# Expert layer walked by pairs of units, with a second place for five of the twelve weight panels

## The chip, the cores and the metric

The program runs on one core of one Trainium2 chip. The metric is the time of one execution on the device, in microseconds (us). The number to forecast is the time of the changed kernel beside a median of 2511.3 us for the kernel before.

## The reference, cut to what matters

The program computes three transformer blocks in a row on 256 tokens of width 1024, in float32. The change lies in the second block, in its mixture of experts. Each token picks 4 of 32 experts; an expert is a pair of dense layers with a clipped gate between them:

```
logits = h @ router_w + router_b
top_logit, top_idx = top_k(logits, 4);  gate = softmax(top_logit)
# for each expert e and the tokens that picked it
hid = xb @ w1[e] + b1[e]                  # [tokens, 2048]
glu = minimum(hid[:, :1024], 7.0)
lin = clip(hid[:, 1024:], -7.0, 7.0)
act = glu * sigmoid(1.702 * glu) * (lin + 1.0)
out = (act @ w2[e] + b2[e]) * gate        # summed into each token's row
```

## The kernel before

**Units.** A unit is up to 64 tokens of one expert. Every expert has one unit; an expert with more than 64 tokens gets further units behind the first 32. With these inputs no expert has more, so 32 units run, unit u being expert u. The number of units and their experts are computed on the chip, so each engine first reads a small table, `unit_int`, into a register, and then runs a hardware loop over units (`Fori`).

**Panels.** The weights of an expert are 12 panels of 1 MB each (128 partitions of 8 KB): panels 0 to 7 are `w1`, panels 8 to 11 are `w2`. Each panel has one place: panels 0 to 5 lie in `core.ring`, panels 6 to 11 in `expert_ring`. SyncE (SP) issues all panel transfers, in order, on one queue. For panel j of unit u it waits until TensorE has used panel j of unit u-1 (semaphore `used`), and ahead of each unit it reads the expert's number from the table. TensorE waits for `loaded[j]` ahead of panel j. The twelve panels of expert 0 are fetched earlier, by `load_first`, which SP runs at the end of the block of the output projection (`linear` with `w_out2`); the last four of these wait for that projection's own last panels.

**A unit on TensorE** (line numbers of the profile): the bias (L2599); 32 matmuls with panels 0 to 7 (L2604), 64 tokens as the stationary side, so that two matmuls lie beside each other in the two column halves; `scatter` of the unit before (L2413), which brings the outputs back to their tokens; `gather` of the tokens of the next unit (L2386); turning of the gates (L2613); turning of the hidden values (L2618), which needs a copy by ScalarE to have freed its PSUM bank; bias (L2623), which needs VectorE's first `add`; turning of the gathered tokens (L2392); 16 matmuls with panels 8 to 11 (L2634). After the last unit `scatter` runs once more, and VectorE adds it and updates the residual `x`.

**Scatter before.** `ytok` holds the unit's output with its first 512 columns on partitions 0 to 63 and its last 512 on 64 to 127. `selt` is 128 x 512: the gates stand in the upper left and the lower right block and zeros elsewhere, so four matmuls of 128 rows by 512 columns bring both halves at once, into banks 2 to 5.

**Order.** All order is written by hand. Engines meet at the ends of blocks (`core.block()`), where every engine waits for the others. An fp32 matmul stands in the trace as two records, each with a weight load of its own.

Of the kernel before, what the change touches and what calls it, by code (L numbers as in the profile page):

```python
# [14 lines left out]
P = 128  # L15
TOK = 256
NB = TOK // P
D = 1024
# [2309 lines left out]
def mixture_of_experts(core, h, norm, bias, ring, rw):  # L2328
# [6 lines left out]
    with ExitStack() as s:  # L2335
# [6 lines left out]
        unit_int = sb("unit_int", [1, MAX_UNITS + 1], I32)  # L2342
        selt, ytok = sb("selt", [P, 2 * TOK]), sb("ytok", [P, D // 2])
# [3 lines left out]
        xt, xg, hidt = sb("xt", [P, D // 2]), sb("xg", [P, 4, 2, S]), sb("hidt", [P, D // 2])  # L2347
        glu, lin, sg = sb("glu", [P, D // 2]), sb("lin", [P, D // 2]), sb("sg", [P, D // 2])
        loaded, used = ring.loaded, ring.used
# [6 lines left out]
        scatter_banks = (2, 3, 4, 5)  # L2356

        def unit_count(eng):
            return eng.value_load(unit_int[0:1, MAX_UNITS:MAX_UNITS + 1], min_val=E, max_val=MAX_UNITS)
# [43 lines left out]
        def scatter(pe, u):  # L2403

            pe.wait_ge(copied.sem, copied.at(u))
            pe.wait_ge(gates_copied.sem, gates_copied.at(u))

            pe.wait_ge(added.sem, added.at(u * 4))  # L2410
            for t, bank in enumerate(scatter_banks):

                pe.matmul(ps[:, bank, :], ytok[:, t * P:t * P + P], selt[:, :], start=True, stop=True).then_inc(scattered.sem, 1)  # L2413

        def add(dve, u):
            for t, bank in enumerate(scatter_banks):
                dve.wait_ge(scattered.sem, scattered.at(u * 4 + (t + 1)))
                dve.tensor_tensor(acc[:, t::4, :], acc[:, t::4, :],  # L2418
                                  ps[:, bank, :].rearrange("p (k n) -> p k n", n=TOK), ALU.add).then_inc(added.sem, 1)

        with ExitStack() as s2:
# [9 lines left out]
            row = sb2("row", [1, MAX_UNITS + 1])  # L2431
# [4 lines left out]
            with core.block() as block:  # L2436
# [66 lines left out]
                def _(dve):  # L2503
# [61 lines left out]
                    link(dve.tensor_scalar(row[:, MAX_UNITS:], cum[0:1, E - 1:E], float(E), None, ALU.add))  # L2565
# [10 lines left out]
        with core.block() as block:  # L2576
            @block.sync
            def _(sp):
                n = unit_count(sp)
                with sp.Fori(1, n) as u:  # L2580
                    e = sp.value_load(unit_int[0:1, bass.ds(u, 1)], min_val=0, max_val=E - 1)
                    for j in range(PANELS):

                        sp.wait_ge(used.sem, u * PANELS - (PANELS - 1 - j))
                        sp.dma_start(ring.panel(j), ring.weights(e, j)).then_inc(loaded[j].sem, 16)

            @block.tensor
            def _(pe):
                n = unit_count(pe)
                with pe.Fori(0, n) as u:  # L2590
                    def panel(j):
                        pe.wait_ge(loaded[j].sem, loaded[j].at(u * 16 + 16))
                        return ring.flat(j)
                    pe.wait_ge(expert_picked.sem, expert_picked.at(u + 1))
                    pe.wait_ge(xg_ready.sem, xg_ready.at(u + 1))

                    for bank in range(2):
                        for out, at in halves:
                            pe.matmul(ps[out, bank, :], pick[:, :], bias[:, bank * D + at:bank * D + at + 512], start=True, stop=False)  # L2599
                    for j in range(8):  # L2600
                        w = panel(j)
                        for bank in range(2):
                            for out, at in halves:
                                mm = pe.matmul(ps[out, bank, :], xg[:, j % 4, j // 4, :], w[:, bank * D + at:bank * D + at + 512],  # L2604
                                               start=False, stop=(j == 7))
                        mm.then_inc(used.sem, 1)
                    scatter(pe, u)

                    pe.wait_ge(picked.sem, picked.at(u + 2))
                    gather(pe)  # L2610
                    pe.wait_ge(gates_picked.sem, gates_picked.at(u + 1))
                    for b in range(NB):
                        mm = pe.transpose(ps[:, 7, b * P:b * P + P], selg[:, b, :], ident)  # L2613
                    mm.then_inc(gates_turned.sem, 1)
                    pe.wait_ge(hid_ready.sem, hid_ready.at(u + 1))
                    pe.wait_ge(xt_ready.sem, xt_ready.at(u + 2))
                    for c in range(4):
                        mm = pe.transpose(ps[:, 6, c * P:c * P + P], lin[:, c * P:c * P + P], ident)  # L2618
                    mm.then_inc(hid_turned.sem, 1)

                    pe.wait_ge(added.sem, added.at(u * 4 + 1))
                    for out, at in halves:
                        mm = pe.matmul(ps[out, 2, :], pick[:, :], bias[:, 2 * D + at:2 * D + at + 512], start=True, stop=False)  # L2623
                    mm.then_inc(bias_used.sem, 1)
                    pe.wait_ge(gates_copied.sem, gates_copied.at(u + 1))
                    turn_gathered(pe, u + 2)
                    pe.wait_ge(hid_copied.sem, hid_copied.at(u + 1))
                    for q in range(4):
                        w = panel(8 + q)
                        for i in range(2):  # L2630
                            k = 2 * q + i
                            at_k = k % 4 * P + k // 4 * S
                            for out, at in halves:
                                mm = pe.matmul(ps[out, 2, :], hidt[:, at_k:at_k + S], w[:, i * D + at:i * D + at + 512],  # L2634
                                               start=False, stop=(k == DT - 1))
                        mm.then_inc(used.sem, 1)
                scatter(pe, n)

            @block.scalar
            def _(act):  # L2640
                n = unit_count(act)
                with act.Fori(0, n) as u:
                    act.wait_ge(glu_ready.sem, glu_ready.at(u + 1))
                    act.activation(sg[:, :], glu[:, :], ACT.Sigmoid, scale=SWIGLU_ALPHA).then_inc(sig_ready.sem, 1)  # L2644
                    copy_gathered(act, u + 2)
                    act.wait_ge(hid_turned.sem, hid_turned.at(u + 1))
                    act.activation(hidt[:, :], ps[:, 6, :], ACT.Copy).then_inc(hid_copied.sem, 1)
                    copy_turned(act, u + 2)

            @block.vector  # L2650
            def _(dve):
                n = unit_count(dve)
                with dve.Fori(0, n) as u:
                    link = LoopChain(turn, dve, u, 5)

                    dve.wait_ge(gathered.sem, gathered.at(u + 1))
                    pick_tokens(dve, link, u + 1)
                    dve.wait_ge(used.sem, used.at(u * PANELS + 8))
                    dve.tensor_scalar(glu[:, :], ps[:, 0, :], SWIGLU_LIMIT, None, ALU.min).then_inc(glu_ready.sem, 1)  # L2659
                    link(dve.tensor_scalar(lin[:, :], ps[:, 1, :], SWIGLU_LIMIT, -SWIGLU_LIMIT, ALU.min, ALU.max))  # L2660
                    dve.wait_ge(glu_ready.sem, glu_ready.at(u + 1))
                    link(dve.scalar_tensor_tensor(out=lin[:, :], in0=lin[:, :], scalar=1.0, in1=glu[:, :], op0=ALU.add,
                                                  op1=ALU.mult))
                    dve.wait_ge(sig_ready.sem, sig_ready.at(u + 1))
                    link(dve.tensor_tensor(lin[:, :], lin[:, :], sg[:, :], ALU.mult))
                    dve.sem_inc(hid_ready.sem, 1)
                    dve.wait_ge(gates_turned.sem, gates_turned.at(u + 1))
                    dve.tensor_copy(selt[0:S, 0:TOK], ps[0:S, 7, 0:TOK])
                    dve.tensor_copy(selt[S:P, TOK:], ps[S:P, 7, 0:TOK]).then_inc(gates_copied.sem, 1)
                    add(dve, u)  # L2670
                    pick_gates(dve, link, u + 1)
                    dve.wait_ge(bias_used.sem, bias_used.at(u + 1))
                    pick_expert(dve, u + 1)
                    dve.wait_ge(used.sem, used.at(u * PANELS + 12))
                    dve.tensor_copy(ytok[:, :], ps[:, 2, :]).then_inc(copied.sem, 1)  # L2675
                    link.done()
# [653 lines left out]
```

## Time and profile before

| what | value |
|---|---|
| median of three runs | 2511.3 us (2507.07 to 2517.31) |
| the profiled execution's own time | 2518.12 us |
| its span, first to last instruction | 2515.1 us |
| TensorE busy | 2374.4 us, 94% of the span |
| VectorE, ScalarE, GpSimd busy | 680.9, 411.7, 66.0 us |
| mean granted TensorE clock | 0.975 of full speed |
| moved from HBM | 616.63 MB, 246 GB/s over the span |

The time is that of an execution, the span lies within it, 3 us shorter. Busy shares are means over stages of quite different kinds: three blocks of dense layers, and between about 1275 and 2234 us the expert loop, some 38% of the whole. A share of the whole span says nothing of what limits the loop; that is read from windows within it.

### The profile page before, as it was taken

How to read it: one execution, taken by the hardware profiler on the slowest of the kernel's cores; microseconds unless marked ns; L12 is line 12 of the kernel's file. 1: busy time of each engine (PE TensorE's matmuls, PEld its weight loads, DVE VectorE, ACT ScalarE, POOL GpSimd, SP SyncE). 2: the span in 40 equal slices, each digit the busy share in tenths (PEclk: the TensorE clock that was granted, in tenths of full speed). 3: DMA queues.
4: the chain of work that ended last, by engine and by line, in shares of the span. 5: the costliest groups of instructions: out<-in, count | busy, mean ns of one | idle time of the engine just before them, and what ended most of it. 6: DMA issues, size and time to landing. Idle time of an engine off the chain costs nothing. (4 is left out here: it accounts for less than half of the span.)

```text
span 2515.1 us, 31570 instructions
## 1 busy us (share of the span) xinstructions
PE 2374.4 (94%) x12727; PEld 1548.0 (62%) x12727; DVE 680.9 (27%) x1486; ACT 411.7 (16%) x837; POOL 66.0 (3%) x72
## 2 busy tenths in 40 slices
PE   8999999999999998997789999999999999989998
PEld 7778788886788877875633333333333333348787
DVE  3142100025200024525222232222222222242322
ACT  2210100014100013223311111111111111112331
POOL 0110000000000000011200000000000000000000
PEclk9999999999999999998789999999999999989999
DMA  6333544455744444300569999999999999952422
GB/s 258 117 117 134 201 151 142 159 201 218 284 167 147 146 159 159 118 19 1 222 242 417 418 418 418 418 417 417 417 417 418 418 418 417 418 224 92 152 76 91
DMA packets 105015, 619.00 MB, mean 246 GB/s; under 512 B 9856, under 2 KB 11136, under 8 KB 48128
## 3 DMA queue, kind: packets, MB, share of 16 engines
q1 hardware_dynamic: 103216, 611.10, 62.1%
q10 hardware_dynamic: 1712, 6.63, 0.7%
q8 instruction: 69, 1.13, 0.2%
q14 instruction: 18, 0.15, 0.0%
HBM read 616.63 MB, written 1.05 MB: 246 GB/s over the span
## 5 line engine op out<-in xcount | busy, mean ns | idle before, releaser
L391 PE MATMUL ps<-x_res,ring 128*128 128x256 f32 x2560 | 568.2, 383 | 21.6 <-ACT x_res L953 12.9
L391 PEld LDWEIGHTS ps<-x_res,ring 128*128 128x128 f32 x2560 | 488.2, 192 | 97.7 <-issue 22.4
L2604 PE MATMUL ps<-ring,moe_xg 128*64 128x512 f32 x1536 | 336.9, 595 | 0.0
L391 PE MATMUL ps<-first_arena,ring 128*128 128x256 f32 x1088 | 239.4, 379 | 0.5 <-DMA ring<-w_o_dram 0.5
L2604 PEld LDWEIGHTS ps<-ring,moe_xg 128*64 128x64 f32 x1536 | 110.7, 137 | 208.4 <-issue 202.9
L2634 PE MATMUL ps<-expert_ring,moe_hidt 128*64 128x512 f32 x1024 | 226.8, 595 | 0.0
L391 PEld LDWEIGHTS ps<-first_arena,ring 128*128 128x128 f32 x1088 | 206.6, 190 | 29.0 <-DMA ring<-w_o_dram 1.0
L391 PE MATMUL ps<-third_h,ring 128*128 128x256 f32 x768 | 176.6, 387 | 5.2 <-ACT third_h L274 3.9
L391 PEld LDWEIGHTS ps<-third_h,ring 128*128 128x128 f32 x768 | 147.7, 194 | 28.2 <-issue 6.5
L2634 PEld LDWEIGHTS ps<-expert_ring,moe_hidt 128*64 128x64 f32 x1024 | 70.5, 137 | 133.5 <-issue 133.5
L2659 DVE TENSOR_SCALAR moe_glu<-ps 128x512 f32<-128x512 f32 x32 | 22.2, 692 | 417.4 <-PE ps L2604 417.4
L2644 ACT ACTIVATE moe_sg<-moe_glu 128x512 f32<-128x512 f32 x32 | 20.1, 629 | 637.2 <-DVE moe_glu L2659 637.2
L2413 PE MATMUL ps<-moe_selt,moe_ytok 128*128 128x512 f32 x264 | 122.1, 605 | 0.9 <-DVE moe_ytok L2675 0.9
L2604 PE MATMUL ps<-expert_ring,moe_xg 128*64 128x512 f32 x512 | 115.3, 592 | 0.0
L391 PE MATMUL ps<-mix_arena,ring 128*128 128x256 f32 x416 | 96.5, 390 | 3.9 <-ACT mix_arena L274 3.9
L1330 DVE TENSOR_TENSOR first_arena<-first_arena,ps 128x256 f32<-128x256 f32 x44 | 18.5, 421 | 286.7 <-PE ps L391 286.7
L2413 PEld LDWEIGHTS ps<-moe_selt,moe_ytok 128*128 128x128 f32 x264 | 47.4, 189 | 75.1 <-issue 75.1
L391 PEld LDWEIGHTS ps<-mix_arena,ring 128*128 128x128 f32 x416 | 79.9, 195 | 17.2 <-issue 5.7
L2418 DVE TENSOR_TENSOR moe_acc<-moe_acc,ps 128x512 f32<-128x512 f32 x132 | 82.1, 683 | 2.8 <-PE ps L2413 1.8
L2604 PEld LDWEIGHTS ps<-expert_ring,moe_xg 128*64 128x64 f32 x512 | 36.8, 137 | 73.1 <-issue 73.1
L2675 DVE COPY moe_ytok<-ps 128x512 f32<-128x512 f32 x32 | 22.1, 692 | 176.1 <-PE ps L2634 176.1
L2386 PE MATMUL ps<-moe_ht,moe_sel 128*64 128x512 f32 x264 | 65.7, 619 | 1.6 <-DVE moe_sel L2365 1.6
(522 smaller groups left out, 1985.5 us busy)
## 6 DMA issues: line engine op xcount, KB each, us to landing
expert_ring<-w_dram SPq DMA_DIRECT2D x192, 1024.0 KB, 15.1
ring<-w_dram SPq DMA_DIRECT2D x192, 1024.0 KB, 15.9
ring<-w_in_dram SPq DMA_DIRECT2D x55, 1024.0 KB, 4.9
ring<-ffn_up_dram SPq DMA_DIRECT2D x44, 1024.0 KB, 4.9
ring<-ada_dram SPq DMA_DIRECT2D x36, 1024.0 KB, 4.9
ring<-w_out_dram SPq DMA_DIRECT2D x16, 1024.0 KB, 4.9
ring<-ffn_dn_dram SPq DMA_DIRECT2D x16, 1024.0 KB, 4.9
ring<-ple_g_dram SPq DMA_DIRECT2D x8, 1024.0 KB, 7.0
```

Source lines behind the costliest of these rows:

```text
L391: mm = pe.matmul(core.ps[:, t % BANKS, 0:TOK], w[:, k * PANEL + c * P:k * PANEL + c * P + P], sources[panel](k0 + k), start=(k0 + k == 0), ...
L1330: return e.tensor_tensor(h[:, j, :], h[:, j, :], ps, ALU.mult)
L2386: mm = pe.matmul(ps[out, 6, :], sel[:, b, :], ht[:, b, at:at + 512], start=(b == 0), stop=(b == NB - 1))
L2413: pe.matmul(ps[:, bank, :], ytok[:, t * P:t * P + P], selt[:, :], start=True, stop=True).then_inc(scattered.sem, 1)
L2418: dve.tensor_tensor(acc[:, t::4, :], acc[:, t::4, :], ps[:, bank, :].rearrange("p (k n) -> p k n", n=TOK), ALU.add).then_inc(added.sem, 1)
L2604: mm = pe.matmul(ps[out, bank, :], xg[:, j % 4, j // 4, :], w[:, bank * D + at:bank * D + at + 512], start=False, stop=(j == 7))
L2634: mm = pe.matmul(ps[out, 2, :], hidt[:, at_k:at_k + S], w[:, i * D + at:i * D + at + 512], start=False, stop=(k == DT - 1))
L2644: act.activation(sg[:, :], glu[:, :], ACT.Sigmoid, scale=SWIGLU_ALPHA).then_inc(sig_ready.sem, 1)
L2659: dve.tensor_scalar(glu[:, :], ps[:, 0, :], SWIGLU_LIMIT, None, ALU.min).then_inc(glu_ready.sem, 1)
L2675: dve.tensor_copy(ytok[:, :], ps[:, 2, :]).then_inc(copied.sem, 1)
```

## The change

- A loop turn now handles two units, an even and an odd one. The number of turns is the number of units halved and rounded up (three more small operations on VectorE while routing); an odd count would be filled up with an empty unit.
- Panels 0 to 4 have two places, one for even and one for odd units (`expert_ring` grows by five panels). The other seven keep one place.
- `load_first` also fetches panels 0 to 4 of expert 1, as its last five transfers.
- SP's order of transfers: for the units up to 17, panels 0 to 4 of unit u+1 go ahead of panels 5 to 11 of unit u; from there on in the order in which they are used. For the first 32 units SP takes the expert from its loop counter and reads no table.
- `scatter` is eight matmuls of 64 rows by 256 columns without the zeros, four for each row half, each half into banks of its own. `selt` is half as wide and is copied by one VectorE operation instead of two. `add` is four operations as before, on other slices.
- `hidt`, `glu`, `lin` and `sg` now lie in the memory of `h` (`mix2_y`), which is no longer needed there.

```diff
 def add(dve, u):
-    for t, bank in enumerate(scatter_banks):
-        dve.wait_ge(scattered.sem, scattered.at(u * 4 + (t + 1)))
+    for n, (q, i) in enumerate(((0, 0), (0, 1), (1, 0), (1, 1))):
+        part = acc[:, 4 * i + 2 * q:4 * i + 2 * q + 2, :]
...
 # scatter
-            for t, bank in enumerate(scatter_banks):
-                pe.matmul(ps[:, bank, :], ytok[:, t * P:t * P + P], selt[:, :], start=True, stop=True).then_inc(scattered.sem, 1)
+            for t in range(4):
+                for i, (rows, _) in enumerate(halves):
+                    mm = pe.matmul(ps[:, 2 + 2 * i + t // 2, t % 2 * TOK:t % 2 * TOK + TOK], ytok[rows, t * P:t * P + P],
+                                   selt[rows, :], start=True, stop=True)
+                    if t % 2 == 1:
+                        mm.then_inc(scattered.sem, 1)
...
 # routing
-                    link(dve.tensor_scalar(row[:, MAX_UNITS:], cum[0:1, E - 1:E], float(E), None, ALU.add))
+                    link(dve.tensor_scalar(pairs, cum[0:1, E - 1:E], float(E), 0.5, ALU.add, ALU.mult))
+                    link(dve.tensor_scalar(pairs, pairs, 0.25, ROUND, ALU.add, ALU.add))
+                    link(dve.tensor_scalar(pairs, pairs, ROUND, None, ALU.subtract))
+                    link(dve.tensor_scalar(row[:, MAX_UNITS + 1:], pairs, -1.0, None, ALU.add))
...
 # SP
-                with sp.Fori(1, n) as u:
-                    e = sp.value_load(unit_int[0:1, bass.ds(u, 1)], min_val=0, max_val=E - 1)
-                    for j in range(PANELS):
-                        sp.wait_ge(used.sem, u * PANELS - (PANELS - 1 - j))
-                        sp.dma_start(ring.panel(j), ring.weights(e, j)).then_inc(loaded[j].sem, 16)
+                def load(u, turn, panels, odd, e):
+                    for j in panels:
+                        sp.wait_ge(used.sem, turn * PANELS + (j + 1))
+                        sp.dma_start(ring.panel(j, odd), ring.weights(e, j)).then_inc(ring.loaded_at(j, odd).sem, 16)
+                twice, once = range(TWICE), range(TWICE, PANELS)
+                with sp.Fori(1, AHEAD) as v:
+                    load(v * 2, v * 2 - 2, twice, 0, v * 2)
+                    load(v * 2 - 1, v * 2 - 2, once, 1, v * 2 - 1)
+                    load(v * 2 + 1, v * 2 - 1, twice, 1, v * 2 + 1)
+                    load(v * 2, v * 2 - 1, once, 0, v * 2)
+                def in_turn(v, before, even, odd):
+                    load(v * 2 - 1, v * 2 - 2, once, 1, before)
+                    load(v * 2, v * 2 - 2, twice, 0, even)
+                    load(v * 2, v * 2 - 1, once, 0, even)
+                    load(v * 2 + 1, v * 2 - 1, twice, 1, odd)
+                with sp.Fori(AHEAD, E // 2 - 1) as v:
+                    in_turn(v, v * 2 - 1, v * 2, v * 2 + 1)
...
-PANELS = 12
+PANELS, TWICE, AHEAD = 12, 5, 9
...
 # load_first
+        for j in range(TWICE):
+            sp.dma_start(self.panel(j, 1), self.weights(1, j)).then_inc(self.loaded_at(j, 1).sem, 16)
```

On SP, in the block ahead of the routing, stand the transfers of `load_first` (its first two lines are panels 6 and 7, then 8 to 11, then 0 to 5). Before:

```order
L2717 DMA expert_ring<-w_dram 128x2048 x2
L2717 DMA expert_ring<-w_dram 128x2x1024 x4
L2717 DMA ring<-w_dram 128x2048 x6
L364 UNCONDITIONAL_BRANCH
L2577 UNCONDITIONAL_BRANCH
```

And now:

```order
L2762 DMA expert_ring<-w_dram 128x2048 x2
L2762 DMA expert_ring<-w_dram 128x2x1024 x4
L2762 DMA ring<-w_dram 128x2048 x6
L2764 DMA expert_ring<-w_dram 128x2048 x5
L364 UNCONDITIONAL_BRANCH
L2587 UNCONDITIONAL_BRANCH
```

Five transfers stand between the last one that waits for the projection and the end of the block (L364).

On TensorE, the first half of a unit in the loop: bias, panels 0 to 7, `scatter` (L2413), `gather` (L2386). Before:

```order
L2599 MATMUL ps<-bias_parts,moe_pick 64x512 x4
L2592 ISA
L2604 MATMUL ps<-ring,moe_xg 64x512 x24
L2604 MATMUL ps<-expert_ring,moe_xg 64x512 x8
L2410 ISA
L2413 MATMUL ps<-moe_selt,moe_ytok 128x512 x4
```

And now, the odd unit of a turn (bias L2633, panels L2638, `scatter` L2414):

```order
L2633 MATMUL ps<-bias_parts,moe_pick 64x512 x4
L2638 MATMUL ps<-expert_ring,moe_xg 64x512 x20
L2626 ISA
L2638 MATMUL ps<-ring,moe_xg 64x512 x4
L2638 MATMUL ps<-expert_ring,moe_xg 64x512 x8
L2410 ISA
L2414 MATMUL ps<-moe_selt,moe_ytok 128x256 x8
```

The odd unit reads its first five panels (20 matmuls) from `expert_ring`; in the scatter, eight matmuls of 256 columns stand where four of 512 stood.

## Rows read from the trace of the kernel before

**Rows 1.** Timeline of TensorE, one unit: start us, us, engine line op.
```profile
1336.98 10.47 PE L2604 MATMUL ps<-ring,moe_xg 128*64 128x512 f32 x48
...
1350.82 3.70 PE L2413 MATMUL ps<-moe_selt,moe_ytok 128*128 128x512 f32 x8
1354.45 1.94 PE L2386 MATMUL ps<-moe_ht,moe_sel 128*64 128x512 f32 x8
1356.31 0.44 PE L2613 MATMUL ps<-mat,moe_selg 128*128 128x128 f32 x2
1357.17 0.63 PE L2618 MATMUL ps<-mat,moe_lin 128*128 128x128 f32 x4 [0.42 <-ACT moe_xt L2397]
1358.42 0.41 PE L2623 MATMUL ps<-bias_parts,moe_pick 96*64 96x512 bf16 x2 [0.62 <-DVE moe_acc L2418]
...
1359.35 7.09 PE L2634 MATMUL ps<-expert_ring,moe_hidt 128*64 128x512 f32 x32
...
1366.70 10.47 PE L2604 MATMUL ps<-ring,moe_xg 128*64 128x512 f32 x48
```

**Rows 2.** Windows: stretch, us, busy of PE, PEld, DVE, ACT, POOL; PEclk; DMA share; GB/s.
```profile
1280.00:1290.00 10.00, 10.00 (x49) 3.55 (x47) 0.00 (x0) 0.00 (x0) 0.00 (x0) 1.00 0.93 359
...
1300.00:1330.00 30.00, 28.96 (x130) 10.19 (x132) 8.25 (x20) 3.97 (x6) 0.00 (x0) 1.00 0.95 379
...
1400.00:1500.00 100.00, 96.88 (x436) 33.78 (x431) 24.39 (x55) 11.11 (x15) 0.00 (x0) 1.00 1.02 417
...
2210.00:2220.00 10.00, 9.17 (x36) 3.18 (x32) 4.06 (x7) 1.61 (x3) 0.00 (x0) 1.00 0.88 351
```

**Rows 3.** DMA view of 1320 to 1360 us: KB each, median us to landing.
```profile
ring<-w_dram SPq DMA_DIRECT2D x6, 1024.0 KB, 10.6
```

**Rows 4.** DMA view of 2150 to 2198 us, the same columns.
```profile
ring<-w_dram SPq DMA_DIRECT2D x8, 1024.0 KB, 21.2
```

**Rows 5.** Timeline of TensorE, a pair of 64-row matmuls of 256 columns in the first block.
```profile
572.82 0.60 PE L1085 MATMUL ps<-first_arena 64*128 64x256 f32 x4
573.35 2.86 PE L391 MATMUL ps<-x_res,ring 128*128 128x256 f32 x12
```

**Rows 6.** Timeline of the last unit and of what follows it.
```profile
2219.46 2.48 DVE L2418 TENSOR_TENSOR moe_acc<-moe_acc,ps 128x512 f32<-128x512 f32 x4
...
2221.13 7.09 PE L2634 MATMUL ps<-expert_ring,moe_hidt 128*64 128x512 f32 x32
...
2229.09 3.69 PE L2413 MATMUL ps<-moe_selt,moe_ytok 128*128 128x512 f32 x8 [0.87 <-DVE moe_ytok L2675]
2230.24 0.69 DVE L2418 TENSOR_TENSOR moe_acc<-moe_acc,ps 128x512 f32<-128x512 f32 x1 [1.29 <-PE ps L2413]
...
2232.82 0.69 DVE L2418 TENSOR_TENSOR moe_acc<-moe_acc,ps 128x512 f32<-128x512 f32 x1 [0.17 <-PE ps L2413]
```

**Rows 7.** Timeline around the end of the block ahead of the routing.
```profile
1232.70 2.06 SPq L2717 DMA_DIRECT2D ring<-w_dram  x4
1232.71 0.48 DVE L2250 SCALAR_TENSOR_TENSOR x_res<-ps,modulations,x_res 128x256 f32<-128x256 f32 x1 [2.97 <-PE ps L391]
...
1235.60 0.17 DVE L530 SCALAR_TENSOR_TENSOR norm_gain<-modulations,vec 128x8 f32<-128x8 f32 x1 [2.40 <-PEq L364]
```

**Rows 8.** Timeline at the end of the routing and at the loop's entry.
```profile
1271.82 0.14 DVE L2565 TENSOR_SCALAR route_row<-route_cum 1x1 f32<-1x1 f32 x1
1271.99 0.18 DVE L2566 CAST moe_unit_int<-route_row 1x49 int32<-1x49 f32 x1
...
1274.87 1.06 PE L2599 MATMUL ps<-bias_parts,moe_pick 96*64 96x512 bf16 x4 [3.35 <-issue]
```

**Rows 9.** Window of the first block in which TensorE waited and the transfers were saturated, columns as in rows 2.
```profile
620.00:640.00 20.00, 17.70 (x194) 12.29 (x187) 5.36 (x18) 5.34 (x14) 0.00 (x0) 1.00 1.00 397
```

**Rows 10.** The page's DMA queues: packets, MB, share of 16 engines.
```profile
q8 instruction: 69, 1.13, 0.2%
```

**Rows 11.** DMA queues of 1400 to 1600 us; this one alone moves anything there.
```profile
q1 hardware_dynamic: 14771, 83.53, 101.7%
```

More of the change, by code:

```diff
@@ L2587, in _ @@
+                last = sp.value_load(unit_int[0:1, MAX_UNITS + 1:MAX_UNITS + 2], min_val=E // 2 - 1, max_val=MAX_UNITS // 2 - 1)
+                load(last * 2 + 1, last * 2, once, 1, expert(last * 2 + 1))
             @block.tensor
             def _(pe):
[L2589 to L2601, printed above, removed]
+                n = pair_count(pe)
@@ new lines, in _, with panel @@
+                with pe.Fori(0, n) as v:
+                    for odd in range(2):
+                        u = v * 2 + odd
+                        def panel(j):
+                            sig = ring.loaded_at(j, odd)
+                            pe.wait_ge(sig.sem, sig.at((v if j < TWICE else u) * 16 + 16))
+                            return ring.flat(j, odd)
+                        pe.wait_ge(expert_picked.sem, expert_picked.at(u + 1))
+                        pe.wait_ge(xg_ready.sem, xg_ready.at(u + 1))
@@ L2621, in _ @@
[L2621 to L2636, printed above, removed]
@@ L2637, in _ @@
-                scatter(pe, n)
+                                pe.matmul(ps[out, bank, :], pick[:, :], bias[:, bank * D + at:bank * D + at + 512], start=True, stop=False)
+                        for j in range(8):
+                            w = panel(j)
+                            for bank in range(2):
+                                for out, at in halves:
+                                    mm = pe.matmul(ps[out, bank, :], xg[:, j % 4, j // 4, :], w[:, bank * D + at:bank * D + at + 512],
+                                                   start=False, stop=(j == 7))
+                            mm.then_inc(used.sem, 1)
@@ new lines, in _ @@
+                        for c in range(4):
+                            mm = pe.transpose(ps[:, 6, c * P:c * P + P], lin[:, c * P:c * P + P], ident)
+                        mm.then_inc(hid_turned.sem, 1)
+                        pe.wait_ge(added.sem, added.at(u * 4 + 1))
+                        for out, at in halves:
+                            mm = pe.matmul(ps[out, 2, :], pick[:, :], bias[:, 2 * D + at:2 * D + at + 512], start=True, stop=False)
+                        mm.then_inc(bias_used.sem, 1)
@@ L2639, in _ @@
+                scatter(pe, n * 2)
             @block.scalar
             def _(act):
[L2641 to L2648, printed above, removed]
+                n = pair_count(act)
@@ L2650, in _ @@
             @block.vector
             def _(dve):
[L2652 to L2675, printed above, removed]
```

120 lines of the change are left out of this document (85 added, 35 removed).

## The prediction

> **What bounds the kernel now.** I read the page first. Its busy shares say 94% for TensorE, but over the whole span that is a mean of unlike stages, so I went to the expert loop alone, where the diff works: first its windows, then the timeline of one unit, then the DMA view at an early and at a late stretch.
>
> The windows show both sides of the loop full: TensorE busy 96.88 of 100 us at the full clock, DMA share 1.02 at 417 GB/s [rows 2]. Only one of them can set the pace, and the timeline says which. A unit takes 1366.70 - 1336.98 = 29.72 us, and in it TensorE waits for ScalarE (0.42) and VectorE (0.62), never for a panel [rows 1]. So the loop runs at TensorE's pace. The transfers are slower than that: 83.53 MB in 200 us is 417.65 GB/s [rows 11], so a panel of 1.0486 MB takes 2.511 us and twelve take 30.13 us, 0.41 us more than a unit. The DMA view confirms it: a panel lands 10.6 us after its issue early on and 21.2 us after it at the end [rows 3, 4], and 28 units (from the middle of the one stretch to that of the other) by 0.41 make 11.5. A panel's place comes free a whole unit before the panel is needed again, so this growing delay never reached TensorE in 32 units. DMA is the second limit, 1.4% behind the first: whatever TensorE gains is worth only what DMA lets through. That sets the method: find when the last panel would land, and what TensorE must do after it.
>
> **The transfers.** Before: the windows give a start of transfers at 1290 - 3.59 MB/417.65 GB/s = 1281.4 and an end at 2210 + 8.4 = 2218.4, with 30 - 27.2 = 2.8 us empty between 1300 and 1330 [rows 2]. From the count, 1281.4 + 2.8 + 372 x 2.511 = 2218.2, so the price of a panel holds over the loop. After the change 367 panels are left, five having been fetched in a stretch that has no transfers. The first new transfer still waits for TensorE's first use of panel 0, so the start stays. The 2.8 us hole came from panels 8 to 11, whose places come free late in unit 0; now five panels for unit 2, which have a place at once, stand ahead of them in the queue, so I take the hole as filled. Afterwards SP's next panel always has a free place: with DMA setting the pace, a single place is free when its unit ends, some 15 us after the landing of panel 7, and its next transfer begins 20 us or more after that landing. The loop's 921.4 us of transfers run through.
>
> **Scatter.** It takes 1354.45 - 1350.82 = 3.63 us now [rows 1]. The new form, 64 rows by 256 columns in fp32, one matmul per row half, does occur in this trace: four records, a pair of matmuls, take 573.35 - 572.82 = 0.53 us with the switch to the next form [rows 5]. A 512-column matmul of the old kind takes 3.63/4 = 0.91, so 256 columns one after the other would be 0.45 each and 0.91 a pair; 0.53 shows the halves running beside each other. Four pairs cost between 4 x 0.43 (half of the old work, 0.85 us being the 512-column step without its share of the switch) and 4 x 0.53, so 1.7 to 2.1; I take 1.85, nearer the lower end, because the switch is paid once. Gain 1.78. VectorE then needs one copy instead of two ahead of the first add, and the 0.62 us wait at L2623 shrinks by 0.43. From the start of scatter to L2634 the time goes from 1359.35 - 1350.82 = 8.53 to 6.32 us, the unit from 29.72 to 27.5. That is below the 30.13 of DMA. TensorE starts with a lead of about 17 us at panel 5 (unit 1's panel 5 is the sixth in the new order and lands at 1281.4 + 6 x 2.511 = 1296.5; TensorE, 2.2 us earlier than before, wants it at 1336.98 - 29.72 - 2.2 + 5 x 1.73 = 1313.7), loses 2.6 us of it in each unit, and waits for panels from about unit 8 on. Of the 2.2 x 32 = 71 us that scatter takes off TensorE, most turn into such waits.
>
> **The end of the loop.** The last panel lands at 1281.4 + shift + 921.4. Panel 7 lands four panels earlier (10.04); after it TensorE needs 1.73 for the panel (13.84 us for eight, by the starts at 1336.98 and 1350.82 [rows 1]), 6.32 to L2634 and 7.09 for L2634. Panels 8 to 11 land meanwhile and hold nothing up. So L2634 ends 5.1 us after the last landing. It now ends at 2221.13 + 7.09 = 2228.2 [rows 6]. Behind it, last scatter and adds take 2232.82 + 0.69 - 2229.09 = 4.42; now the first add can again begin after 1.15 (two pairs instead of one matmul of twice the width), and four adds take 2.48 [rows 6]: 3.6, a gain of 0.8.
>
> **What the change costs ahead of the loop.** SP's last four transfers of `load_first` are released by the projection's last panel and take until 1232.70 + 2.06 = 1234.76. VectorE is done at 1233.19, yet the next block starts at 1235.60 [rows 7]: the block's end waits for SP. Five more issues stand there, at (2.06 - 0.35)/3 = 0.57 us each (0.35 for the last one's own length, my estimate), so 2.9 us on the path. If the meeting of the engines hid them it would be 0; at 2.06/3 each it would be 3.4. I take 2.9, since the three moments fit nothing else. Three more linked operations on one element at 1271.99 - 1271.82 = 0.17 [rows 8] add 0.5. Together a shift of 3.4 us for all that follows. The five panels land while nothing else is fetched, 25 us before unit 1.
>
> **Parts at nothing.** SP's table reads: each panel lands 10 to 21 us after issue [rows 3, 4], so SP is that far ahead; without that cover a read would stand between two panels. The half as wide clearing of `selt` on GpSimd ends long before the loop. New memory for `hidt`, `glu`, `lin`, `sg`: same operations. The order for units up to 17 changes which panel is waited for, not how many come: a gap saved there is spent before the end.
>
> **The sum.** Last landing 1281.4 + 3.4 + 921.4 = 2206.2; end of L2634 2211.3 against 2228.2, -16.9; tail -0.8; together -17.7 us. The profiled execution took 2518.1, so 2500.4 for it; it was 6.8 us above the median of the runs shown, so I put the same difference to the median: 2511.3 - 17.7 = **2493.6 us**.
>
> **The rivals.**
> *Transfers get slower* (the other side). All now hangs on the price of a panel, which was covered before. With deeper queues and no slack, every 1% costs 9.2 us. At 2.559 us a panel (410 GB/s) the gain is gone; at the 397 GB/s of a saturated stretch of the first block [rows 9] a panel takes 2.641, and 367 x 0.130 = 48 us more give 2541. Against it: rate and share stayed the same in this loop while the landing time doubled.
> *The doubled loop body no longer stays in instruction memory.* TensorE's turn holds 256 records before and 544 after (two units, eight more each), and a fetch of instructions is 1.13 MB/69 = 16 KB [rows 10]. Before, none is fetched in the loop [rows 11]. A stall of s at each of 16 turns is hidden up to 60.3 - 55 = 5 us once DMA sets the pace, but TensorE alone would end at 2228.2 + 3.4 - 71 + 16 s: from s = 3.2 on it costs, 4.2 takes the whole gain, and 6 gives 2511.3 + 28.4 - 0.8 = 2539. The whole entry to the loop, table read included, shows 3.35 us [rows 8], so even that bound costs little: 2497.
> The Trainium skill's page Runtime: NRT & Kernel Launch, section Instruction fetch mechanics, speaks against the change here: a taken branch to code outside a window of two pages must fetch its page before going on. It also gives TensorE room for 2048 instructions, by which 544 would fit and s would be 0; no row here shows either.
> *The clock falls in the waits.* TensorE will wait 2.6 us in each 30. At half clock a unit would take 55 us, 25 over DMA's time, so two such units would make the kernel slower, ten would give about 2740. In a stretch with the same kind of waits, TensorE busy 17.70 of 20 us, the granted clock was 1.00 [rows 9].
> The page TensorE: Matmul & The Clock Gate, section Loop structure matters more than you think, warns that waits for DMA between bursts send the clock to half; the row above speaks against it for waits this short.
> *The row halves don't overlap.* Then the unit falls by 0.43 only, to 29.3, TensorE stays the bound, and the end is 2228.2 + 3.4 - 14 = 2217.6: -10.6, 2500.7, no measurable change.
> *More gain.* The issues of SP off the path give 2490.7; a panel 1% cheaper, which a queue that is never short could bring, 2484.4.
>
> **How the numbers follow.** Chances: forecast 0.66; slower transfers 0.10; refetching 0.05; clock 0.03; no overlap 0.05; more gain 0.11. A measurement of this kernel tells 0.5%, 12.6 us, from no change, and -17.7 is only 5 us beyond that, half a percent of the panel's price, so a fifth of the likeliest case may fall short: same 0.20. Faster 0.69, slower 0.11. The range 2479 to 2509 holds the forecast with a panel's price 1% off either way, the case without overlap and most of the gain cases, and leaves out the slow ones.
>
> **What would show it.** In the changed profile: DMA share 1.02 at about 418 GB/s from 1285 to 2206 without the dip near 1300; units of 27.5 us at first and of 30.1 from about the eighth on, with waits for panels under 1 us each and the clock at 1.00; scatter at 1.85 us; the last landing near 2206 and L2634's end 5 us later; the block after `load_first` starting near 1238.5. I am wrong if the rate in the loop is under 414 GB/s, if TensorE never waits for panels, or if a gap of several us opens once per turn.

## The result and the profile after

The changed kernel took a median of 2500.65 us (11 runs, 2496.9 to 2504.47) beside 2516.35 us for the kernel before (11 runs, 2507.07 to 2521.91). The ratio is 0.9934, with a 95% interval from 0.9923 to 0.9944: 14 to 19 us less, 16.6 by the ratio and 15.7 by the medians. It is faster by 0.56 to 0.77%. The forecast was 17.7 us less. Its 2493.6 us lies 7 us under the measured time: 5 of these come from the kernel before, which had a median of 2511.3 us in the three runs shown and 2516.35 in eleven, and 2 from a gain that is 2 us smaller by the medians.

The page of the changed kernel, span and costliest groups of the loop (line, engine, names, count, busy time and mean, idle time before them and what ended it):

```profile
span 2501.1 us, 31823 instructions
...
q8 instruction: 71, 1.16, 0.2%
...
L2638 PE MATMUL ps<-expert_ring,moe_xg 128*64 128x512 f32 x1152 | 262.4, 596 | 24.6 <-DMA expert_ring<-w_dram 24.4
...
L2638 PE MATMUL ps<-ring,moe_xg 128*64 128x512 f32 x896 | 202.9, 598 | 15.5 <-DMA ring<-w_dram 14.9
```

The first of the two groups on the page of the kernel before (the second has 0.0 idle time there too):

```profile
L2604 PE MATMUL ps<-ring,moe_xg 128*64 128x512 f32 x1536 | 336.9, 595 | 0.0
```

TensorE is now idle for 40.1 us ahead of its panels, and 39.3 of these are waits that the landing of a panel ends. Before there was none. The windows, with the columns of [rows 2]:

```profile
1280.00:1290.00 10.00, 10.00 (x42) 3.40 (x40) 0.00 (x0) 0.00 (x0) 0.00 (x0) 0.88 0.58 211
...
1300.00:1330.00 30.00, 29.46 (x152) 11.19 (x152) 9.96 (x24) 4.33 (x7) 0.00 (x0) 1.00 0.99 393
1400.00:1500.00 100.00, 95.42 (x481) 35.30 (x478) 28.63 (x64) 12.26 (x18) 0.00 (x0) 1.00 1.02 417
2200.00:2210.00 10.00, 9.14 (x52) 4.21 (x54) 6.12 (x13) 2.42 (x4) 0.00 (x0) 1.00 0.95 381
```

The rate of the transfers in the middle of the loop is what it was. The timeline of TensorE, first an early unit, then a late one (in brackets the idle time before a row and what ended it):

```profile
1322.30 2.00 PE L2414 MATMUL ps<-moe_selt,moe_ytok 64*128 64x256 f32 x16
1324.22 1.94 PE L2386 MATMUL ps<-moe_ht,moe_sel 128*64 128x512 f32 x8
...
1327.64 0.41 PE L2657 MATMUL ps<-bias_parts,moe_pick 96*64 96x512 bf16 x2
...
1328.56 7.09 PE L2668 MATMUL ps<-expert_ring,mix_y 128*64 128x512 f32 x32
...
1574.42 1.94 PE L2638 MATMUL ps<-ring,moe_xg 128*64 128x512 f32 x8 [0.94 <-DMA ring<-w_dram]
1576.90 1.94 PE L2638 MATMUL ps<-expert_ring,moe_xg 128*64 128x512 f32 x8 [0.55 <-DMA expert_ring<-w_dram]
1579.42 1.94 PE L2638 MATMUL ps<-expert_ring,moe_xg 128*64 128x512 f32 x8 [0.58 <-DMA expert_ring<-w_dram]
...
1604.57 1.94 PE L2638 MATMUL ps<-ring,moe_xg 128*64 128x512 f32 x8 [0.91 <-DMA ring<-w_dram]
```

Scatter lasts 1.92 us by its starts (3.63 in [rows 1]), VectorE's wait at L2657 is gone, and from scatter to L2668 it is 6.26 us. Late, a unit takes 1604.57 - 1574.42 = 30.15 us, with three waits for panels in it, at the last three of the eight; an early one takes 27.45 us. The first wait for a panel comes at 1458.78, in unit 6 counted from 0. The last unit and what follows, the counterpart of [rows 6]:

```profile
2200.38 1.94 PE L2638 MATMUL ps<-expert_ring,moe_xg 128*64 128x512 f32 x8 [0.56 <-DMA expert_ring<-w_dram]
...
2208.52 7.09 PE L2668 MATMUL ps<-expert_ring,mix_y 128*64 128x512 f32 x32
2216.47 2.00 PE L2414 MATMUL ps<-moe_selt,moe_ytok 64*128 64x256 f32 x16 [0.87 <-DVE moe_ytok L2712]
```

And the end of the block ahead of the routing with the loop's entry, the counterpart of [rows 7, 8]:

```profile
1235.72 0.48 DVE L2250 SCALAR_TENSOR_TENSOR x_res<-ps,modulations,x_res 128x256 f32<-128x256 f32 x1 [2.97 <-PE ps L391]
1237.71 2.63 SPq L2764 DMA_DIRECT2D expert_ring<-w_dram  x5
1240.87 0.17 DVE L530 SCALAR_TENSOR_TENSOR norm_gain<-modulations,vec 128x8 f32<-128x8 f32 x1 [4.66 <-PEq L364]
...
1278.80 1.06 PE L2633 MATMUL ps<-bias_parts,moe_pick 96*64 96x512 bf16 x4 [3.93 <-issue]
```

Ahead of all that the diff touches, this execution is already 3.0 us behind the one of before (the last L2250 at 1235.72 against 1232.71). The code there is the same, and in the profiles of the experiments this point moves between 1225.7 and 1237.3, so all comparisons of traces start from it. From it to L2668's end the changed kernel takes 979.89 us, the one before 995.51: -15.6. The tail adds -0.8 (the four adds now end 3.65 us after the last scatter begins, 4.42 before). With -0.6 us behind these adds and the +3.0 ahead, that is the -14.0 between the spans.

### The profile page after: what moved, and what is told of

Its sections match the earlier page's. It is cut to its first block and busy times, and to the rows that moved or that the text cites. A ratio compares the mean times of both kernels' runs of the same rounds, so it can differ in the third digit from the quotient of the medians.

```text
span 2501.1 us, 31823 instructions
## 1 busy us (share of the span) xinstructions
PE 2333.7 (93%) x12991; PEld 1541.4 (62%) x12991; DVE 664.8 (27%) x1457; ACT 391.4 (16%) x821; POOL 65.9 (3%) x72
## 5 line engine op out<-in xcount | busy, mean ns | idle before, releaser
L2638 PE MATMUL ps<-expert_ring,moe_xg 128*64 128x512 f32 x1152 | 262.4, 596 | 24.6 <-DMA expert_ring<-w_dram 24.4
L2668 PE MATMUL ps<-expert_ring,mix_y 128*64 128x512 f32 x1024 | 226.8, 595 | 0.0
L2638 PE MATMUL ps<-ring,moe_xg 128*64 128x512 f32 x896 | 202.9, 598 | 15.5 <-DMA ring<-w_dram 14.9
L2638 PEld LDWEIGHTS ps<-expert_ring,moe_xg 128*64 128x64 f32 x1152 | 77.9, 136 | 198.3 <-issue 126.3
L2668 PEld LDWEIGHTS ps<-expert_ring,mix_y 128*64 128x64 f32 x1024 | 70.6, 137 | 133.4 <-issue 133.4
L2638 PEld LDWEIGHTS ps<-ring,moe_xg 128*64 128x64 f32 x896 | 62.6, 137 | 146.0 <-issue 103.9
L2697 DVE TENSOR_SCALAR mix_y<-ps 128x512 f32<-128x512 f32 x32 | 22.1, 692 | 473.1 <-PE ps L2638 473.1
L2680 ACT ACTIVATE mix_y<-mix_y 128x512 f32<-128x512 f32 x32 | 20.2, 630 | 713.9 <-DVE mix_y L2697 713.9
L2414 PEld LDWEIGHTS ps<-moe_selt,moe_ytok 64*128 64x128 f32 x528 | 48.3, 186 | 32.1 <-issue 27.7
L2386 PE MATMUL ps<-moe_ht,moe_sel 128*64 128x512 f32 x264 | 65.7, 619 | 1.6 <-DVE moe_sel L2365 1.6
L2414 PE MATMUL ps<-moe_selt,moe_ytok 64*128 64x256 f32 x528 | 65.9, 389 | 0.9 <-DVE moe_ytok L2712 0.9
```

The source lines that it names most:

```text
L2386: mm = pe.matmul(ps[out, 6, :], sel[:, b, :], ht[:, b, at:at + 512], start=(b == 0), stop=(b == NB - 1))
L2414: mm = pe.matmul(ps[:, 2 + 2 * i + t // 2, t % 2 * TOK:t % 2 * TOK + TOK], ytok[rows, t * P:t * P + P], selt[rows, :], start=True, stop=True)
```

## The experiments

**The scatter alone, and the places and order alone.** The first kernel is the kernel before with nothing but the new scatter (its matmuls, its copy of `selt` and its `add`):

```diff
-        selt, ytok = sb("selt", [P, 2 * TOK]), sb("ytok", [P, D // 2])
+        selt, ytok = sb("selt", [P, TOK]), sb("ytok", [P, D // 2])
...
-                pe.matmul(ps[:, bank, :], ytok[:, t * P:t * P + P], selt[:, :], start=True, stop=True).then_inc(scattered.sem, 1)
+                for i, (rows, _) in enumerate(halves):
+                    mm = pe.matmul(ps[:, 2 + 2 * i + t // 2, t % 2 * TOK:t % 2 * TOK + TOK], ytok[rows, t * P:t * P + P],
+                                   selt[rows, :], start=True, stop=True)
...
```

> The kernel before with the new scatter, selt copy and add only: one place for each panel, no extra panels fetched early, single units. If the loop is now set by transfers (my theory), 372 panels still have to land by about 2218 us, so the gain is only what lies behind the last landing: 2218.4 + 6.5 against 2228.2, and 0.8 in the tail, about -4 us against the kernel before (ratio 0.998), with TensorE waiting for panels in late units. Rival 1: scatter is the whole gain and the second places are idle: -16 us. Rival 2: with one place for each panel the waits of TensorE hold places back and the transfers tear: no gain or slower.

Measured 2510.44 us, ratio 0.9971 (0.9961 to 0.9981): -7.3 us, 3 us more than I had put down. Its trace shows 1.4 of these: between 1290 and 1330 us 1.2 us of transfers are missing, in the kernel before 2.6. The rest is within the interval. The lines of TensorE in its loop:

```profile
L2609 PE MATMUL ps<-ring,moe_xg 128*64 128x512 f32 x1532 | 346.2, 597 | 17.0 <-DMA ring<-w_dram 13.8
...
L2609 PE MATMUL ps<-expert_ring,moe_xg 128*64 128x512 f32 x504 | 120.4, 602 | 27.8 <-DMA expert_ring<-w_dram 27.8
```

So it waits for panels like the changed kernel, with single places. The second kernel is the changed one with the old scatter (the same edit the other way round).

> The changed kernel with the old scatter (four matmuls of 128 rows by 512 columns, two selt copies). My theory: TensorE sets the pace again at 29.7 us a unit, panels fetched early buy nothing, and what remains is the price ahead of the loop, some 2.3 us for five issues and 1 us in routing and loop entry: +3 us against the kernel before (ratio 1.001). Rival: the second places and the new order shorten the loop by themselves: -12 us.

Measured 2518.51 us, ratio 1.0002 (0.9993 to 1.0011), with no wait for a panel in the loop. The +3 us that I had expected is not there: the loop's entry lies 43.09 us behind the last L2250, 42.16 in the kernel before, because the block behind the longer gap is shorter (see the last section). Alone the places and the order bring nothing; alone the scatter brings 7.3 us; together they bring 16.6. With the old scatter TensorE sets the pace, and five panels fewer in the loop are worth nothing. With the new one the transfers set it, and those five (5 x 2.51 = 12.6 us) lie on the path. The step from the scatter alone to both is 9.3 us by the ratios and 10.8 by the traces to the end of L2668, less than 12.6: the transfers start 0.6 us later, 0.5 us more are missing near 1300, and what is left would be a slightly higher price of a panel.

**Where the five extra transfers are issued.** The third kernel issues them ahead of the six that wait for the projection:

```diff
-        for j in [*range(RING, PANELS), *range(RING)]:
...
+        for j in range(RING, PANELS):
             sp.dma_start(self.panel(j), self.weights(0, j)).then_inc(self.loaded[j].sem, 16)
         for j in range(TWICE):
             sp.dma_start(self.panel(j, 1), self.weights(1, j)).then_inc(self.loaded_at(j, 1).sem, 16)
+        for j in range(RING):
+            sp.wait_ge(core.panel_used.sem, core.panel_used.at(range(j, total, RING)[-1] + 1))
+            sp.dma_start(self.panel(j), self.weights(0, j)).then_inc(self.loaded[j].sem, 16)
```

> The changed kernel, but load_first issues the five panels of expert 1 ahead of the six that wait for the projection instead of behind them. My theory: the block's end waited for those five issues, and the whole rest of the program moves up by their 2.3 us: -18 us against the kernel before, 2.3 us less than the changed kernel. Rival: the block's end waits for something else, or the early transfers hold back the bias and router loads: same as the changed kernel, about -15.7.

Measured 2498.33 us, ratio 0.9927 (0.9913 to 0.994). By the time alone, 1.8 us less by the ratios, it can't be told from the changed kernel (0.9923 to 0.9944). The trace does tell: from the last L2250 to the next block 1236.33 - 1234.05 = 2.28 us, against 5.15 after and 2.89 before. The entry comes 3.0 us earlier (40.05 us behind the last L2250, 43.08 after) and the end of L2668 3.6 us earlier. The fourth kernel goes further: the six panels of the ring are issued in the routing's block, where nothing has to be waited for; `load_first` issues only the other eleven.

```diff
+    def load_more(self, sp):
+        for j in range(RING):
+            sp.dma_start(self.panel(j), self.weights(0, j)).then_inc(self.loaded[j].sem, 16)
...
+                @block.sync
+                def _(sp):
+                    ring.load_more(sp)
```

> As the run before, and in addition the six panels of expert 0 that go into ring are issued without a wait in the routing block, so that SP is done early in the projection's block. My theory: the block's end then waits for VectorE alone (1233.2 + 0.35 in the trace of before, where it was 1235.6): 2 us more, -20 us against the kernel before. The six panels need 15 us and have 40. Rival: the issues in the routing block or their transfers delay the loop's entry: no better than -16.

Measured 2493.4 us, ratio 0.9909 (0.9894 to 0.9925), the fastest version: 6.3 us less than the changed kernel by the ratios, whose intervals just touch. Its timeline:

```profile
1232.96 0.48 DVE L2250 SCALAR_TENSOR_TENSOR x_res<-ps,modulations,x_res 128x256 f32<-128x256 f32 x1 [2.97 <-PE ps L391]
1233.80 2.98 SPq L2767 DMA_DIRECT2D ring<-w_dram  x6
1233.84 0.17 DVE L530 SCALAR_TENSOR_TENSOR norm_gain<-modulations,vec 128x8 f32<-128x8 f32 x1 [0.40 <-PEq L364]
...
1234.38 3.72 PE L517 MATMUL ps<-mix_y,mat 128*128 128x256 f32 x16 [1.46 <-ACT mix_y L524]
```

The gap is 0.88 us, and L517's 16 records take 3.72 us instead of 5.40. From the last L2250 to the loop's entry (1270.30) it is 37.34 us, against 43.08 after: 4.3 from the gap, 1.5 from the block behind it, where TensorE's clock stood higher in L517 (see the last section). Inside the loop 0.9 us is lost again (937.75 us from the entry to the end of L2668, 936.81 after).

**The order of the transfers.** The fifth kernel fetches in order of use from the start, the sixth keeps the order by free places up to unit 3 instead of up to unit 17 (AHEAD = 2 instead of 9). The edit of the fifth:

```diff
-                with sp.Fori(1, AHEAD) as v:
-                    load(v * 2, v * 2 - 2, twice, 0, v * 2)
-                    load(v * 2 - 1, v * 2 - 2, once, 1, v * 2 - 1)
-                    load(v * 2 + 1, v * 2 - 1, twice, 1, v * 2 + 1)
-                    load(v * 2, v * 2 - 1, once, 0, v * 2)
...
-                with sp.Fori(AHEAD, E // 2 - 1) as v:
+                with sp.Fori(1, E // 2 - 1) as v:
```

> The changed kernel with SP's loads in order of use from unit 1 on; two places and the five panels fetched early stay. My theory: the order is worth what it does at the start. The first load is now panel 5 of unit 1, whose place comes free five panels (8.7 us) later than that of panel 0, and panels 8 to 11 are again waited for late in unit 0 (2 to 3 us empty): about +11 us against the changed kernel, -5 against the kernel before. Rival: transfers catch up, because only their total counts and the order costs nothing: -16.

Measured 2509.85 us, ratio 0.9967 (0.9956 to 0.9979): +8.3 us beside the changed kernel. Entry and SP's first rows:

```profile
1275.05 1.07 PE L2627 MATMUL ps<-bias_parts,moe_pick 96*64 96x512 bf16 x4 [3.89 <-issue]
...
1288.00 0.35 SPq L2593 DMA_DIRECT2D ring<-w_dram  x1
```

Panel 5 of unit 1 stands first now, and its place comes free only after TensorE's panel 5: SP starts 12.95 us after the entry instead of 1283.09 - 1278.80 = 4.29. That is 8.7 us. The second part of the expectation is there too: from 1290 to 1330 us 4.4 us of transfers are missing, 1.7 after. By the traces, from the last L2250 to the last L2668's end, the loss is 11.5 us (991.41 against 979.89), the sum of the two. The 8.3 us of the ratios is lower, but their intervals leave about 4 us either way.

> The changed kernel with the order by free places for units up to 3 only (AHEAD 2), in order of use from there. My theory: the order counts only at the start, so this is the changed kernel, -16 us against the kernel before. Rival: the order keeps the transfers full through the first 17 units: several us slower.

Measured 2506.06 us, ratio 0.9956 (0.9942 to 0.997). I had expected no loss; the rival of my expectation came true. A window and SP's row show it:

```profile
1340.00:1360.00 20.00, 19.52 (x104) 7.70 (x102) 6.66 (x14) 2.42 (x4) 0.00 (x0) 1.00 0.76 294
...
1343.07 0.37 SPq L2593 DMA_DIRECT2D ring<-w_dram  x1
```

At the switch SP stood at panel 5 of unit 3, which has one place, until 1343.07, when TensorE had used it. At 294 GB/s the window is 20 x (1 - 294/417) = 5.9 us short of full, and the loss is 5.9 by the traces to L2668's end and 5.5 by the ratios. The changed kernel issues past the same switch at 1757.5 us, when TensorE already waits for panels and the transfers lie some 20 us behind their issue, and no window of 20 us between 1760 and 1820 falls below 415 GB/s.

**How many panels have two places.** Two instead of five (TWICE = 2), so 370 panels in the loop instead of 367, and three issues fewer ahead of it.

> The changed kernel with two places for panels 0 and 1 only, and two panels fetched early. My theory: each panel fetched early is worth its 2.51 us and costs one issue of 0.46 us ahead of the routing, so three fewer give +7.5 - 1.4 = +6.1 us against the changed kernel, -10 against the kernel before; with two panels ahead the hole near 1300 us may be deeper, 1 to 2 us more. Rival: it is the second place that keeps the transfers running, and fewer of them cost much more than their own transfers: +15 or more.

Measured 2508.46 us, ratio 0.9964 (0.9954 to 0.9974): +7.6 beside the changed kernel, and 3 x 2.51 = 7.5. The gap at the block's end fell to 3.68 us, but the entry stayed where it was (43.11 us behind the last L2250, 43.08 after), so the 1.4 us that I had set against the 7.5 did not come, and neither did a deeper hole near 1300.

**The table reads.** SP reads the expert of each unit from the table again, as before.

```diff
+                    before, even, odd = expert(v * 2 - 1), expert(v * 2), expert(v * 2 + 1)
...
```

> The changed kernel, but SP reads the experts' numbers from the table in every loop turn. My theory: SP runs 10 to 20 us ahead of the landings, so nothing changes: -16 us against the kernel before. Only the reads ahead of the first load could show, and they lie within the wait for TensorE's first panel. Rival: reads leave holes between transfers: some 1 us for each of 15 turns, +15.

Measured 2502.25 us, ratio 0.9938 (0.9919 to 0.9956). No difference to the changed kernel that can be measured, and SP's first issue follows the entry by 4.30 us, 4.29 after.

**Which of the two sets the pace.** The last two kernels take work off one side each. The first leaves out half of the scatter's matmuls:

```diff
-            for t in range(4):
+            for t in (1, 3):
```

> The changed kernel with the odd two of the four pairs of scatter's matmuls alone (each about 0.48 us in a unit of TensorE): half of the outputs are left out. Theory, the transfers set the pace after about the seventh unit: TensorE's work in the middle of the loop is covered, and only what it leaves out behind the last landing counts, 1 us in the last unit and 1 us in the last scatter; the waits for panels grow by 1 us a unit. About -2 us beside the changed kernel, 2498, -18 beside the kernel before. Rival, TensorE's work still counts in each unit: 32 x 1 us, 2469.

Measured 2498.48 us, ratio 0.9921 (0.9895 to 0.9947). The interval holds the changed kernel's ratio and is far from the 0.98 of the rival. Entry to L2668's end takes 934.43 us, against 936.81 after, although each unit has 0.9 us less to do. Of these 2.4 us about 1 is the last unit's own, as expected, and 1.4 are the smaller hole near 1300 (0.3 us of transfers missing, 1.7 after). Its late units show where the rest of the saving went:

```profile
2157.46 1.94 PE L2638 MATMUL ps<-ring,moe_xg 128*64 128x512 f32 x8 [0.23 <-DMA ring<-w_dram]
...
2187.62 1.94 PE L2638 MATMUL ps<-expert_ring,moe_xg 128*64 128x512 f32 x8 [0.25 <-DMA expert_ring<-w_dram]
```

These are two units, 30.16 us apart as before, each now with five waits instead of four in the same late units (panel 3's, shown, is the new one). In all, TensorE waits 61.0 us for panels, 39.3 after.

The second fetches only half of each panel in the loop, the other half stays that of an earlier expert:

```diff
+                        place, source = ring.panel(j, odd), ring.weights(e, j)
+                        if j < 8:
+                            place, source = place[:, 0:1024], source[:, 0:1024]
+                        else:
+                            place, source = place[:, 0:1, :], source[:, 0:1, :]
...
```

> The changed kernel with only half of each panel fetched in the loop (half of the weights are those of an earlier expert), so the same number of transfers, waits and issues with half the bytes. Theory, the price of a panel is the bytes and it alone sets the pace: TensorE never waits for a panel, its units stay at 27.45 us to the end, and the loop ends at 1279 + 32 x 27.45 = 2157 us in place of 2215: about -57 us beside the changed kernel, 2444, ratio to the kernel before 0.971. Rival, the waits come from something else in the transfers (their issue by SP, the hand-over of places): units stay near 30.1 us and the time near 2500. Rival, TensorE's own pace is slower than the early units show when all their panels lie there: anything between.

Measured 2438.6 us, ratio 0.9697 (0.9656 to 0.9737). The last unit, a window, and the lines of the loop:

```profile
2141.86 7.09 PE L2673 MATMUL ps<-expert_ring,mix_y 128*64 128x512 f32 x32
...
1400.00:1500.00 100.00, 98.56 (x496) 36.66 (x496) 25.75 (x62) 10.69 (x16) 0.00 (x0) 1.00 0.67 225
...
L2643 PE MATMUL ps<-expert_ring,moe_xg 128*64 128x512 f32 x1152 | 255.3, 592 | 0.0
```

No wait for a panel is left, with the same number of transfers, issues and hand-overs. Entry (1268.59) to L2673's end (2148.95) takes 880.4 us, 27.5 for each of 32 units; the 56.4 us to the changed kernel's 936.8 are what its waits for bytes cost. That is more than the 40.1 of idle time on the page, because a wait costs more than its idle time: with a wait ahead of each panel, TensorE takes a panel every 1.94 + 0.55 = 2.49 us instead of 1.73, which is 0.76 for a wait of 0.55.

## Why the prediction was right, and where it was not

**Right.** Halving the bytes removed all waits; halving the scatter moved L2668's end by 2.4 us and otherwise only lengthened the waits. Scatter cost 1.92 us (1.85). Table reads cost nothing that can be measured. The moved buffers were not tested alone, but the units took what was forecast with them. The three more operations on one element cost 0.5. The waits began in unit 6, where the forecast had about unit 8.

**The terms, from the last L2250 on.** They are worked out from the bytes of windows of one trace of each kernel. The last landing is at 2209.1 (if the window 2200 to 2210 is full up to there), the first transfer starts at 1290 - 2.11 MB/417 GB/s = 1284.95. The last landing came 12.3 us earlier than before, against 12.2 in the forecast, but by other numbers:

| term, us against before | forecast | measured |
|---|---|---|
| start of the transfers | +3.4 | +0.5 |
| five panels fewer | -12.6 | -12.6 |
| hole near 1300 | -2.8 | -1.1 |
| price of a panel (2.514 for 2.511) | 0 | +1.0 |
| L2668's end behind the last landing | -4.7 | -3.3 |
| tail | -0.8 | -0.8 |
| sum | -17.7 | -16.4 |

(The terms are rounded, and the forecast's own count of the transfers before ended 0.2 us under the end that it read, so the columns add up to -17.5 and -16.3.) The sum is close partly by luck: the start came out 2.9 us cheaper than forecast, and hole, price and end together 4.1 us dearer.

*Start, mis-sized.* The five issues of SP lengthened the gap at the block's end by 2.26 us (2.9 forecast): each took 0.57, but SP was done only 2.57 us later than before, and the hand-over behind it was 0.31 us shorter. Then TensorE ran through L517 and the router's matmuls 1.9 us faster than before, at a higher clock, and gave most of it back. The 0.5 us of the three operations came as forecast, and SP's first issue followed the loop's entry 0.4 us sooner (4.29 us for 4.66). The forecast had neither the 1.9 nor the 0.4.

*Hole, partly wrong.* "I take the hole as filled" failed: 1.7 us are missing, most of them here:

```profile
1305.00:1310.00 5.00, 5.00 (x28) 1.80 (x26) 1.19 (x4) 0.00 (x0) 0.00 (x0) 1.00 0.89 273
```

The five panels for unit 2 fill 12.6 us, and the ninth transfer would start at 1284.95 + 8 x 2.51 = 1305.0. It is panel 8 of unit 1, whose place TensorE frees at about 1301.1 + 1.7 = 1302.8. SP issues it at 1303.23, and the first transfer started 1.86 us after its issue (1283.09 to 1284.95), which gives 1305.1 here: the margin is gone. With half a scatter, when TensorE reaches L2668 0.8 us earlier behind the entry, the window 1300 to 1330 has 413 GB/s and 0.3 us are missing. That fits a hole, not its size, and no run was made for this alone.

*End, mis-sized.* The 5.1 us of the forecast left no time between the last byte of panel 7 and its first use. That landing is at 2209.1 - 10.05 = 2199.05 and TensorE begins at 2200.38: 1.33 us.

**Wrong in its reason.** "The order for units up to 17 changes which panel is waited for, not how many come: a gap saved there is spent before the end" was put at nothing. A gap in the transfers is not got back, even when it falls into the early units in which TensorE still sets the pace, because the transfers set the end; and the order decides whether there is one: 11.5 us by the trace (8.3 by the ratios) in order of use from the start, 5.9 (5.5) with the switch at unit 3. The number came out right only because the forecast had SP never waiting for a place, which is what this order achieves.

**The rivals.** *Slower transfers*: the panel's price rose by 0.003 us, a tenth of a percent. *Refetching of the doubled body*: no gap per turn; the page has 71 packets of instructions against 69 in [rows 10], one of the two comes between 1295 and 1325 us, in the first turn, and from 1400 to 2200 us queue q8 moves nothing. The rule of the Trainium skill that spoke against the change (page Runtime: NRT & Kernel Launch, section Instruction fetch mechanics) has no effect visible here at 544 records a turn. *Clock in the waits*: 1.00 with 2.1 us of waits for panels in 30. The warning in the Trainium skill about long waits for DMA between matmuls (page TensorE: Matmul & The Clock Gate, section Loop structure matters more than you think) did not come true for waits of at most 0.94 us. *No overlap of row halves*: 0.48 us a pair, so they overlap. *More gain*: its first half, SP's issues off the path, is real, and the fourth kernel has it. Its second half, a cheaper panel, did not come.

## What to carry to other kernels

When two limits lie 1.4% apart, a large saving on the first is soon cut off by the second: the scatter's 2.2 us in each of 32 units, 71 us of TensorE, gave 7.3 alone. Work out both ends, the last landing and what must follow it, and the gain is their sum. Then every byte and every gap in the second limit is on the path: prefetch during stretches that fetch nothing, and order transfers by free places until the queue leads. From there the order of use did no harm; whether going back to it is needed, no run tests. Transfers issued by an engine at the end of a block hold up all engines: put them into the next block if nothing there needs them at once.

## What the runs showed of the hardware

The block between L530 and the loop's entry does the same work in all kernels, but for 0.5 us of operations, and its length goes with the length of the stop ahead of it. Gap from the last L2250 to L530, TensorE's idle time before L517, time of L517, and L530 to the entry:

| kernel | gap | idle | L517 | block |
|---|---|---|---|---|
| before | 2.89 | 3.46 | 6.53 | 39.27 |
| ring issued in routing | 0.88 | 1.46 | 3.72 | 36.46 |
| extra issued early | 2.28 | 2.85 | 5.14 | 37.77 |
| two panels twice | 3.68 | 4.26 | 6.12 | 39.43 |
| after | 5.15 | 5.72 | 5.40 | 37.93 |

The six other kernels with a gap of 5.1 to 5.3 have blocks of 37.9 (37.85 to 37.90), and the scatter alone, with before's gap, has 39.3. The windows over L517 alone, first of the version with the ring issued in routing, then of before and of after, give the granted clock (third figure from the right, in parts of 2.4 GHz):

```profile
1234.38:1238.10 3.72, 3.72 (x16) 2.95 (x16) 0.00 (x0) 2.09 (x7) 1.94 (x3) 1.00 1.04 390
```

```profile
1236.10:1242.60 6.50, 6.47 (x16) 4.95 (x16) 0.00 (x0) 2.13 (x7) 2.18 (x3) 0.56 1.02 425
```

```profile
1241.40:1246.80 5.40, 5.40 (x16) 4.19 (x16) 0.00 (x0) 2.10 (x7) 1.94 (x3) 0.68 1.03 428
```

After 1.46 us idle TensorE kept its full 2.4 GHz through L517; in the others it stood at 1.2 for most of it. The router's matmuls behind it took 8.70 us at 0.50 before (from 1246.57) and 7.90 us at 0.56 after (from 1250.71). Up to 3.5 us of idle time L517 got slower with the length of the stop, at 4.3 and 5.7 quicker again. Why is open; no run tests it. It moves the block by up to 3 us here, as much as the term that it followed.

Row halves of 64 rows by 256 columns in fp32 cost 1.92/4 = 0.48 us a pair, beside 0.91 for a 512-column matmul of 128 rows. By the working above, a panel's last byte and its first use lie 1.3 us apart. An issue on SP takes 0.57 us in a row of several.
